# Interleaving four chunks of a delta-rule recurrence and placing half of the head pairs on the other partitions

## What is computed

```python
def step(state, inp):
    r_t, w_t, k_t, v_t, kk_t, b_t = inp
    sa = jnp.einsum('bhvk,bhk->bhv', state, -kk_t)
    state = (state * w_t[:, :, None, :] + sa[..., None] * b_t[:, :, None, :]
             + v_t[..., None] * k_t[:, :, None, :])
    return state, jnp.einsum('bhvk,bhk->bhv', state, r_t)
```

## Time and profile before

| | |
|---|---|
| median of 3 runs | 3126.95 us (3126.18 to 3134.32) |
| the profiled execution's span, first to last instruction | 3129.4 us |
| TensorE matmul, busy | 2931.8 us (94%) |
| TensorE weight loads, busy | 1889.1 us (60%) |
| VectorE / ScalarE / GpSimd busy | 1556.1 / 957.6 / 637.5 us |
| granted TensorE clock, mean | 0.979 |
| stage of the recurrence, in the span | 1285 to 1830 us |

### The profile page before, as it was taken

The page is one execution under the profiler, slowest core; times in us unless marked ns, Lnnn a source line. Parts: engine busy times, 40 slices in busy tenths (PEclk is TensorE's granted clock), DMA queues, the critical chain, the costliest instruction groups (busy, mean ns, idle before and its releaser), DMA issues. The chain is left out here.

```text
span 3129.4 us, 66008 instructions
## 1 busy us (share of the span) xinstructions
PE 2931.8 (94%) x25434; PEld 1889.1 (60%) x25435; DVE 1556.1 (50%) x3592; ACT 957.6 (31%) x2271; POOL 637.5 (20%) x780
## 2 busy tenths in 40 slices
PE   8999999999969999799999989997699999999999
PEld 6778877777746666688888855554233333333333
DVE  4676767677778889433333357775111111111111
ACT  3343334333447777322222223332000000000000
POOL 0000000000035555200000000001233333333333
PEclk9999999999989999899999999998799999999999
DMA  7121111112131000411111113335498878776763
GB/s 241 61 70 62 62 62 63 61 58 73 61 104 41 28 15 1 142 37 45 45 45 37 37 55 108 108 95 202 126 328 295 301 273 320 281 272 251 254 238 120
DMA packets 190197, 397.46 MB, mean 127 GB/s; under 512 B 16155, under 2 KB 76443, under 8 KB 188913
## 3 DMA queue, kind: packets, MB, share of 16 engines
q1 hardware_dynamic: 169440, 343.47, 31.7%
q0 software_dynamic: 20512, 50.54, 4.7%
HBM read 327.25 MB, written 80.32 MB: 130 GB/s over the span
## 5 line engine op out<-in xcount | busy, mean ns | idle before, releaser
L325 PE MATMUL pj_big<-pj_xnT,pj_w_in 128*128 128x256 f32 x2816 | 634.8, 381 | 4.6 <-ACT pj_ubuf L397 3.0
L325 PEld LDWEIGHTS pj_big<-pj_xnT,pj_w_in 128*128 128x128 f32 x2816 | 537.4, 191 | 85.7 <-ACT pj_ubuf L397 6.9
L1810 PE MATMUL ex_pgu<-keep_res,ex_xT 128*64 128x512 f32 x2560 | 568.9, 597 | 0.0
L1810 PEld LDWEIGHTS ex_pgu<-keep_res,ex_xT 128*64 128x64 f32 x2560 | 177.1, 137 | 334.9 <-issue 334.9
L1918 DVE TENSOR_TENSOR ex_hh<-ex_sg,ex_pgu 128x256 f32<-128x256 f32 x80 | 33.7, 421 | 584.0 <-ACT ex_sg L1883 584.0
L1828 PE MATMUL ex_py<-keep_res,ex_hT 128*64 128x512 f32 x1280 | 288.3, 592 | 1.0 <-DVE ex_yb L1926 1.0
L758 POOL TENSOR_SCALAR at_tt<-at_e,at_cf 128x512 f32<-128x512 f32 (+3 forms) x160 | 219.3, 1374 | 185.7 <-DVE at_pd L802 163.5
L1329 PE MATMUL mg_po<-keep_res,mg_mix 128*128 128x512 f32 x512 | 234.1, 614 | 7.0 <-DVE mg_mix L1632 7.0
L737 ACT ACTIVATE at_e<-at_sc,at_nmx 128x512 f32<-128x512 f32 (+3 forms) x320 | 196.9, 623 | 68.9 <-DVE at_nmx L780 66.6
L295 POOL TENSOR_TENSOR pj_m<-pj_qn,pj_cosin 128x256 f32<-128x256 f32 x64 | 46.6, 728 | 827.6 <-DVE pj_qn L524 601.4
L1883 ACT ACTIVATE ex_sg<-ex_pgu 128x256 f32<-128x256 f32 x80 | 30.7, 384 | 582.5 <-PE ex_pgu L1810 582.5
(11 more groups left out here) (293 smaller groups left out, 4720.1 us busy)
## 6 DMA issues: line engine op xcount, KB each, us to landing
keep_res<-in_w_exp_gate SPq DMA_DIRECT2D x32, 2048.0 KB, 8.6
keep_res<-in_w_exp_up SPq DMA_DIRECT2D x32, 2048.0 KB, 15.5
keep_res<-in_w_exp_down SPq DMA_DIRECT2D x32, 2048.0 KB, 8.6
chunks_s<-pj_st SPq DMA_DIRECT2D x32, 642.0 KB, 4.0
rw_raw<-chunks_s SPq DMA_DIRECT2D x32, 642.0 KB, 3.9
pj_xt<-in_x SPq DMA_DIRECT2D x20, 512.0 KB, 3.8
qk_s<-pj_qo SPq DMA_DIRECT2D x64, 128.0 KB, 1.9
mg_xin<-in_x SPq DMA_DIRECT2D x8, 1024.0 KB, 7.1
```

The source lines that it names most:

```text
L325: ins = pe.matmul(out, lhs, rhs, start=(k == 0), stop=(k == KC - 1))
L1810: ins = pe.matmul(pgu[j * BT:(j + 1) * BT, :, :], lhs, wgu[x][:, k, :, j * HE:(j + 1) * HE], start=(k == 0), stop=(k == KC - 1))
```

## The change

It rewrites `recur`; the other stages stay as they are.

- Four chunks are in work in one turn k: S (chunk k) does the serial part, B (k+1) joins blocks and prepares s0, A (k+2) inverts 16x16 blocks and turns to tokens, N (k+3) does gl and gb. There are 35 turns in place of 33 halves, the first three and the last three of them with a part of the work.
- In pairs 2 and 3, what has tokens on its partitions (`gl`, `gb`, `gk`, `q`, `w`, `tbk`, `tv`, `sa`) lies in the other partition half than the channels of the same head. A product from channels to tokens or back then reads one half and writes the other in these pairs.
- `every` now runs pairs (0, 2) and then (1, 3), and makes no `s_apart` step.
- PSUM is four tiles of two banks, pairs 0 and 1 in the first bank, 2 and 3 in the second. A turn permutes the four.
- The product `gk` times `tv` leaves s1 and becomes s0, a turn earlier; s1 adds to it. r2's wide product becomes two narrow ones, r2q and r2p, and VectorE's copy of `lu4` goes (ScalarE copies both halves, 512 wide, in place of 256). y2 and y3 become one.
- `gl`, `gb`, `gk`, `tbk`, `tv` have four buffers each, the state has two.
- SyncE loads chunks straight into five `cin` buffers, five ahead of the next stage's loads; GpSimd copies nothing.

```diff
-PE_ORDER = ("gl", "gb", "s1", "r1", "s2", "r2", "tok", "r3", "s3", "r4", "y1", "r5", "y2", "r6", "y3", "r7", "gk", "r8")
-ACT_ORDER = ("s1", "r1", "s2", "r2", "tok", "r3", "r5", "y3", "r7")
-DVE_ORDER = ("gl", "gb", "r2", "r3", "r4", "s3", "r6", "gk", "r8")
+PE_TURN = (("s1", 0), ("gl", 3), ("r1", 2), ("gb", 3), ("s2", 0), ("r5", 1), ("r2q", 2), ("r2p", 2), ("s3", 0), ("r6", 1),
+           ("tok", 2), ("r3q", 2), ("r3l", 2), ("r7", 1), ("y1", 0), ("r4", 2), ("y2", 0), ("r8", 1), ("s0", 1), ("gk", 2))
+ACT_TURN = (("s1", 0), ("r1", 2), ("s2", 0), ("r5", 1), ("r2p", 2), ("tok", 2), ("r3l", 2), ("r7", 1), ("y", 0))
+DVE_TURN = (("gl", 3), ("gb", 3), ("w0", 3), ("r2q", 2), ("s3", 0), ("r6", 1), ("st", 0), ("r3q", 2), ("r4", 2), ("r8", 1),
+            ("gk", 2))
+AHEAD = 3
+RING = 4
+LOADS = 5
...
-        ps = [m.ps(f"ps{n}", [P, 512]) for n in range(8)]
+        ps = [m.ps(f"ps{n}", [P, NPAIR, 4 * C]) for n in range(4)]
...
+        def token_half(p, r):
+
+            return HALVES[r] if p < NPAIR // 2 else HALVES[1 - r]
+
+        def banks(k):
+
+            a, b, c, d = 0, 1, 2, 3
+            for _ in range(k + AHEAD):
+                a, b, c, d = d, a, c, b
+            return ps[a], ps[b], ps[c], ps[d]
...
+            for c in range(LOADS, NCH):
+                sp.wait_ge(s_pe, on_pe["y1", c - LOADS])
+                sp.wait_ge(s_dve, on_dve["st", c - LOADS])
+                sp.dma_start(cin[c % LOADS][:, :, :], dr["chunks"][c]).then_inc(s_ld[c % LOADS], 16)
...
+                for j in range(NPAIR // 2):
+                    for f in products:
+                        for p in (j, j + NPAIR // 2):
+                            for r in range(2):
+                                ins = f(p, HALVES[r], token_half(p, r))
+                ins.then_inc(s_pe, 1)
...
+                if live(S_):
+                    if S_ > 0:
+                        pe.wait_ge(s_dve, on_dve["st", S_ - 1])
+                    pe.wait_ge(s_pe, on_pe["s0", S_])
+                    every(lambda p, r, t: product(ba[t, p, LO], xs[r, p, A], state[S_ % 2][r, p, :], False, not first(p)))
...
+                if live(S_):
+                    pe.wait_ge(s_dve, on_dve["r8", S_])
+                    pe.wait_ge(s_act, on_act["s1", S_])
+                    every(lambda p, r, t: product(ba[t, p, LO], q5[S_ % 2][t, p, :], sa0[t, p, :]))
...
+                    every(lambda p, r, t: product(bc[t, p, 0:C], xa[r, p, B], eye[r, :]),
+                          lambda p, r, t: product(bc[t, p, C:2 * C], xa[r, p, K], eye[r, :]),
+                          lambda p, r, t: product(bc[t, p, 2 * C:3 * C], xa[r, p, V], eye[r, :]))
...
+                    pe.wait_ge(s_dve, on_dve["gk", B_])
+                    pe.wait_ge(s_act, on_act["tok", B_])
+                    if live(A_):
+                        pe.wait_ge(s_dve, on_dve["r4", A_])
+                    k0, v0 = gk[B_ % RING], tv[B_ % RING]
+                    every(lambda p, r, t: product(bd[t, p, LO], k0[t, p, LO], v0[t, p, :], first(p), False))
```

More of the change, by code:

```diff
@@ L810, in _, with counts @@
             ch.end("attend, VectorE")
-SERIAL = ("s1", "s2", "s3", "y1", "y2", "y3")
-PE_ORDER = ("gl", "gb", "s1", "r1", "s2", "r2", "tok", "r3", "s3", "r4", "y1", "r5", "y2", "r6", "y3", "r7", "gk", "r8")
-ACT_ORDER = ("s1", "r1", "s2", "r2", "tok", "r3", "r5", "y3", "r7")
-DVE_ORDER = ("gl", "gb", "r2", "r3", "r4", "s3", "r6", "gk", "r8")
[L820 to L833, removed]
+PE_TURN = (("s1", 0), ("gl", 3), ("r1", 2), ("gb", 3), ("s2", 0), ("r5", 1), ("r2q", 2), ("r2p", 2), ("s3", 0), ("r6", 1),
[6 more added lines that the diff above has]
+LOADS = 5
+def counts(turn):
+    order = [(name, k + ahead) for k in range(-AHEAD, NCH) for name, ahead in turn if 0 <= k + ahead < NCH]
+    return {key: n + 1 for n, key in enumerate(order)}
 def recur(nc, io, dr, keep, ahead):
@@ L838, in recur @@
         m = Pool(nc, ctx, "rw")
[L839 to L840 removed]
+        cin = [m.sb(f"cin{n}", [P, NPAIR, ROW]) for n in range(LOADS)]
         eye = m.sb("eye", [P, C])
@@ new lines, in _, with product, every @@
+            A, R, B, K, V = (slice(n * C, (n + 1) * C) for n in range(5))
+            AR = slice(0, 2 * C)
+            def product(out, lhs, rhs, start=True, stop=True):
+                return pe.matmul(out, lhs, rhs, start=start, stop=stop)
+            def every(*products):
+                for j in range(NPAIR // 2):
[4 more added lines that the diff above has]
+                ins.then_inc(s_pe, 1)
@@ L1031, in _, with copy, turn @@
-            half(0, 0, has_serial=False)
-            for c in range(NCH - 1):
-                half(c, c % 2)
-            half(NCH - 1, 1, has_pre=False)
+            def copy(name, c, *pairs):
+                act.wait_ge(s_pe, on_pe["y2" if name == "y" else name, c])
+                for dst, src in pairs:
+                    ins = act.activation(dst, src, ACT.Copy)
+                ins.then_inc(s_act, 1)
+            def turn(k):
+                S_, B_, A_ = k, k + 1, k + 2
+                ba, bb, bc, bd = banks(k)
+                if live(S_):
+                    copy("s1", S_, (sa0[:, :, :], ba[:, :, LO]))
+                if live(A_):
+                    copy("r1", A_, (w2[:, :, :], bc[:, :, PAIR]))
+                if live(S_):
+                    copy("s2", S_, (sa[:, :, :], ba[:, :, LO]))
+                if live(B_):
+                    copy("r5", B_, (ty[0][:, :, :], bb[:, :, PAIR]))
+                if live(A_):
+                    copy("r2p", A_, (w4[:, :, :], bd[:, :, PAIR]))
+                    copy("tok", A_, (tbk[A_ % RING][:, :, :], bc[:, :, PAIR]), (tv[A_ % RING][:, :, :], bc[:, :, 2 * C:3 * C]))
+                    copy("r3l", A_, (l8[:, :, :], ba[:, :, LO]))
+                if live(B_):
+                    copy("r7", B_, (ty[1][:, :, :], bb[:, :, PAIR]))
+                if live(S_):
+                    copy("y", S_, (y[:, :, S_ * C:(S_ + 1) * C], bc[:, :, LO]))
@@ L1076, in _ @@
+            dve.memset(state[0][:, :, :], 0.0).then_inc(s_init, 1)
             dve.wait_ge(s_const, 64)
-            half(0, 0, has_serial=False)
-            for c in range(NCH - 1):
-                half(c, c % 2)
-            half(NCH - 1, 1, has_pre=False)
+            for k in range(-AHEAD, NCH):
+                turn(k)
 NEG = -1e30
```

320 lines of the change are left out of this document (145 added, 175 removed).

## The result

The changed kernel takes **3032.43 us** (median of 4 runs, 3031.0 to 3033.51), the kernel before beside it 3126.56 (4 runs): ratio 0.9698, 95% interval 0.9686 to 0.971. It is faster by 94 us, where 211 were forecast, and lies 27 us above the upper end of the wider range (2898 to 3005). The profiled execution has a span of 3029.8 us at a granted clock of 0.979, as before.

The account below looks back on a forecast made before the run. TensorE was taken to bound the recurrence, through matmul pace and waits. 31 x (16.46 - 9.8) = 206.5, plus 4.3 at the ends, is 210.8 off, giving 2916 us; own range 2898 to 2945.

Parts of the forecast that it names:

- the wider range: Whole kernel: 2898 to 3005 us, covering the forecast and shared pacing up to 25 ns per matmul; chance about 0.8.
- Turn: One chunk's period in the recurrence: 9.52 us of matmul sets, 0.14 wait and 0.13 stalls, 9.8 us against 16.46 before.
- the step on instructions: TensorE's instruction packets in the recurrence: 36 or so per 100 us for 21, costing 4 us at most if stalls doubled.
- the 0.13: Scattered TensorE stalls per recurrence turn, in us: average 16.46 less undisturbed 16.33, kept unchanged in the forecast.
- Rival B: Recurrence: shared issue, instruction supply or SBUF reads pace matmuls at 22 ns; turn 11.6, time 2972 us; chance 0.17.
- Pace of four tiles: Four-tile matmuls in the recurrence run independently, 14.6 ns each; three transpose sets take 0.7 us in place of 1.4.
- C: Recurrence: off-diagonal tiles share the diagonal's pace, so only the waits go; turn 14.0, time 3047 us; chance 0.12.
- D: Recurrence: tiles of the same rows hinder one another, 57 ns per narrow matmul; turn 21.65, time 3284 us; chance 0.04.
- Waits: TensorE's waits for copies in the recurrence: 2.48 us a turn before, hidden by the new order except 0.14.
- The wait forecast before s0: Between r4 and s0 in a turn, y2 and r8 fill 0.70 us of the 0.84 needed: 0.14 us wait.
- The 2.48 us a turn: Rest of the old recurrence turn beyond 13.85 us of matmuls, taken as TensorE waiting for copies, drains included.
- Loads and ends: Chunk loads cost nothing under some 12 us; recurrence ends gain 4.3: 1.3 earlier start, 3 shorter last turns, fill about the same.

## Why the prediction was wrong

**Turn.** Forecast 9.8 us, measured 13.6 (13.30 with the two short turns). The step that failed is the one on instructions: "21 packets of 16 KB come in 100 us; it would be 36 or so. The stalls called issue are 4.1 us in all; doubled they'd cost 4. I keep it inside the 0.13." The packets were counted, but they were taken for a small load that would grow in proportion, not for a stream with a greatest rate. They can't come 36 times in 100 us: at 3.84 us apart there are 26, exactly what the row shows. 4.8 us apart on average, as before, was slow enough to hide that; 2.8 us, which a turn of 9.8 needs, wasn't to be had. The term should have been a bound beside the sum, the turn being the greater of array time and 3.5 packets x 3.84 us = 13.4, in place of "inside the 0.13". Rival B named instruction supply, but as a pace of every matmul, to be seen in a slow set of transposes; it comes as full pace and full stop, and costs more (13.6 for its 11.6). The rival's name fits what was found; its mechanism, its price and its sign do not. In the trace of before, the packets never start less than 3.4 us apart (1330 to 1800): a sign of the bound that the count of 21 in 100 us doesn't show. The case that held neither 22 nor 25 ns but a stop per packet was missing.

**Pace of four tiles.** Right to the digit: 0.70 us for the transposes, and 14.8 ns per matmul in a burst of 128. Rivals C (1.4 us) and D (over 1.8) are excluded by the same row. So is what the prediction took from the Trainium skill (TensorE: Matmul & The Clock Gate), as a rule for four tiles: that a load overlaps only matmuls of another row group (Part 3, "The mechanism"), and that starts keep 25 ns apart ("Wait — 56ns, not 53.3ns?"). But of the 4.4 us a turn that four tiles take off the array, 0.44 came through (0.34 of a full turn).

**Waits.** Right, as far as they can be seen. Without four tiles, the pipeline alone gives 3047.05 us against the 3047 of case C, with TensorE busy 99.9% of 100 us. That both are 3047 is in part luck: the fill was longer and the short turns shorter than forecast (below). The wait forecast before s0 (0.14) can't be seen: TensorE is late for another reason, and no wait for a copy exceeds 2.2 us in all.

**`s_apart`.** Not costed at all ("makes no `s_apart` step" stands in the description of the change, without a term). It is worth 19 us. The 2.48 us a turn that were booked as waits contained it (0.62), and so the sum was not harmed: with the pipeline both go. This is luck.

**Loads and ends.** From 1300 to 1720 TensorE never waits for a chunk (no row of the kind), though the loads stretch the packets by 3%. The fill was sized wrong. The first matmul is at 1288.0, 3.5 us earlier than before, where 1.3 were forecast; but the first state product is at 1317.0, 3.2 us later. The fill takes 29.0 us where it took 22.3, and "about the same" was forecast. The clock isn't the reason: from 1291 to 1304 it is 0.82, where it was 0.50 before. TensorE idles in the fill for 7.0 us called "issue", in three pieces (one window, one row of the timeline):

```profile
1288.00:1317.00 29.00, 20.71 (x593) 19.03 (x597) 9.81 (x18) 6.09 (x12) 0.00 (x0) 0.79 0.92 334
```

```profile
1309.14 0.83 PE L904 MATMUL rw_ps<-rw_eye,rw_cin 64*64 64x64 f32 x29 [3.49 <-issue]
```

The packets of instructions start at 1293.21, 1300.03, 1306.67 and 1313.05, 6.4 to 6.8 us apart in place of 3.84, while the loads of the next stage run at 334 GB/s. In the fill of the other kernels of this pipeline, too, most of these packets stand 6 to 7.6 us apart. So loads can slow the supply by far more than the 3% of the chunk loads; no run took these loads away. At the other end, the two short turns save 7.2 us against full ones, where 3 were forecast, and 4.7 us lie from the last state product to the next stage (1734.08) for the 5.4 of before.

**Where the 94 us come from**, by the ratios to before, in this order: 19 from the increments, 62 from the rest of the pipeline (0.9939 to 0.974), 13 from four tiles (0.974 to 0.9698), each uncertain by 5 to 7 us. Where the other 117 went: 31 x (13.3 - 9.8) = 108 us of waiting for instructions, the rest at the ends.

## What to carry to other kernels

A stream that is written out has a floor that no engine row shows: here 256 instructions per 3.5 to 4 us, some 15 ns per instruction, so 30 ns per pair of load and matmul, and nearly twice that while loads of 334 GB/s ran. Before forecasting a faster small matmul, multiply the instructions of the stretch by that and compare it with the array time; idle time called "issue" in the middle of a set, with a regular spacing, is the sign. Below that floor, gain comes from fewer and wider instructions (columns are free as long as the array's time stays below the floor) or from a loop whose body stays resident (57 KB did, 115 KB didn't); a loop over the turns was not tried here, since the buffers of this pipeline repeat only after more than one turn.

## What the runs showed of the hardware

- Written-out code reaches TensorE in packets of 256 instructions, one under way at a time: 3.74 us apart without chunk loads, 3.84 beside 50 GB/s, 6.4 to 6.8 beside 334 GB/s (fill of the changed kernel). TensorE goes on 1.2 to 1.6 us after a packet has landed (82 of 82 idle pieces).
- A body of 57 KB stays resident in a loop, one of 115 KB does not.
- Four 64x64 tiles of float32 run independently: 14.8 ns per matmul and load in a burst of 128, against 29.2 on the two diagonal tiles.
- Semaphore increments of their own on TensorE's queue cost 69 ns each in the kernel before, waits included (165 us for 72 more a turn), and 12 a turn left out gave back 19 us, 0.62 us a turn. In the changed one 80 more cost 156 us, 61 ns each, at a lower clock.
- Widening four-tile sets from 64 to 128 columns costs next to nothing when they are written out: 960 matmuls take 26.7 us against 26.3.
